# Chunked RWKV-7 recurrence: the 16x16 diagonal blocks of the triangular inverse move from matrix products to a block-per-partition substitution on VectorE, with two more pipeline stages

## The reference

```python
def step(state, inp):
    r_t, w_t, k_t, v_t, kk_t, a_t = inp
    sk = jnp.einsum('bhij,bhj->bhi', state, kk_t)
    state = (state * w_t[:, :, None, :]
             - sk[..., None] * (kk_t * a_t)[:, :, None, :]
             + v_t[..., None] * k_t[:, :, None, :])
    y = jnp.einsum('bhij,bhj->bhi', state, r_t)
    return state, y
```

## Time and profile before

| | |
|---|---|
| median of 3 runs | 3121.45 us (3116.18 to 3122.15) |
| profiled execution, its own time | 3126.26 us |
| span of the profiled execution | 3124.5 us |
| busy in the span: PE, DVE, ACT, POOL | 2800.0, 1582.2, 977.5, 1399.3 us |
| recurrence, from its first to its last work | about 1624 to 2261 us of the span |

### The profile page before, as it was taken

How to read it: one execution, slowest core, us unless ns; L and a number is a source line. 1 busy time by engine, 2 the same in 40 slices (tenths; PEclk the granted TensorE clock), 3 DMA queues, 4 the chain that set the end, 5 groups by cost and what they waited for, 6 DMA issues and landing times. The chain is left out here.

```text
span 3124.5 us, 58516 instructions
## 1 busy us (share of the span) xinstructions
PE 2800.0 (90%) x25184; PEld 2314.8 (74%) x25184; DVE 1582.2 (51%) x1939; ACT 977.5 (31%) x1703; POOL 1399.3 (45%) x742
## 2 busy tenths in 40 slices
PE   1787898999999999898978988888659999999999
PEld 1565676888877887677767887888647888878887
DVE  6744545656536343679635555555313543333344
ACT  2434433222232222445433333333224222222221
POOL 2532244444445444434435555656236444444443
PEclk9889999999999999999989999999879999999999
DMA  6421233544423232465651111111042222222223
GB/s 232 162 74 34 89 128 114 175 162 173 163 82 104 85 101 95 112 166 137 168 142 57 50 54 53 50 50 50 24 120 95 81 101 98 97 95 94 97 99 122
DMA packets 208642, 327.19 MB, mean 105 GB/s; under 512 B 126209, under 2 KB 126337, under 8 KB 208385
## 3 DMA queue, kind: packets, MB, share of 16 engines
q1 hardware_dynamic: 208384, 323.44, 32.5%
HBM read 288.86 MB, written 33.55 MB: 103 GB/s over the span
## 5 line engine op out<-in xcount | busy, mean ns | idle before, releaser
L687 POOL TENSOR_TENSOR wl<-w,wh 128x1024 fp32r<-128x1024 f32 x368 | 905.9, 2468 | 1305.0 <-ACT wh L728 1304.8
L180 PE MATMUL ps<-hi,wh 128*128 128x512 f32 x2208 | 883.8, 400 | 57.4 <-POOL wl L687 42.6
L181 PE MATMUL ps<-lo,wh 128*128 128x512 f32 x2208 | 870.0, 394 | 0.0
L182 PE MATMUL ps<-hi,wl 128*128 128x512 f32 x2208 | 869.5, 394 | 0.0
L728 ACT ACTIVATE wh<-w 128x1024 fp32r<-128x1024 f32 x368 | 388.1, 1056 | 708.3 <-DMA w<-in_ffn_w_in 527.7
L180 PEld LDWEIGHTS ps<-hi,wh 128*128 128x128 f32 x2208 | 420.4, 190 | 159.8 <-POOL wl L687 42.8
L994 DVE SCALAR_TENSOR_TENSOR xt<-ps,mod,xt 128x512 f32<-128x512 f32 x384 | 286.4, 750 | 437.7 <-PE ps L182 437.4
L181 PEld LDWEIGHTS ps<-lo,wh 128*128 128x128 f32 x2208 | 420.7, 191 | 89.5 <-issue 3.7
L182 PEld LDWEIGHTS ps<-hi,wl 128*128 128x128 f32 x2208 | 420.1, 190 | 90.0
L180 PE MATMUL ps<-act_hi,wh 128*128 128x512 f32 x704 | 282.2, 401 | 18.2 <-DVE act_lo L1003 9.7
L999 DVE TENSOR_TENSOR act<-ps,silu 128x512 f32<-128x512 f32 x88 | 60.8, 691 | 467.2 <-PE ps L182 467.2
(11 more groups left out here) (209 smaller groups left out, 3805.4 us busy)
## 6 DMA issues: line engine op xcount, KB each, us to landing
w<-in_ffn_w_in SPq DMA_DIRECT2D x176, 512.0 KB, 3.4
piece<-in_ada_w SPq DMA_DIRECT2D x96, 512.0 KB, 4.8
w<-in_ffn_w_out SPq DMA_DIRECT2D x88, 512.0 KB, 3.3
w<-in_w_rkv SPq DMA_DIRECT2D x48, 512.0 KB, 3.8
scratch<-silu SPq DMA_DIRECT2D x48, 256.0 KB, 2.9
scratch<-act SPq DMA_DIRECT2D x48, 256.0 KB, 2.9
w<-in_wqk SPq DMA_DIRECT2D x20, 512.0 KB, 5.0
xt<-in_xT SPq DMA_DIRECT2D x4, 2048.0 KB, 10.8
```

Of the source, the lines that this page charges most:

```text
L180: pe.matmul(out, w_hi(k), x_hi(k), start=first and k == 0, stop=False)
L181: pe.matmul(out, w_hi(k), x_lo(k), start=False, stop=False)
L182: ins = pe.matmul(out, w_lo(k), x_hi(k), start=False, stop=last and k == kc - 1)
L687: pool.tensor_tensor(wl[n % NW][:, :, :], wr[n % NW][:, :, :], wh[n % NW][:, :, :].bitcast(F32), ALU.subtract).then_inc(*wlo.up)
```

## The change

The inverse of the 16x16 diagonal blocks is no longer found by the levels 1, 2, 4 and 8 on PE. Instead, for chunk d:

- SP stores `n_t` to a DRAM image (`n_blocks`, 2 transfers), and reads the 64 diagonal blocks (16 heads x 4) back so that each lies in one partition of a 64-partition tile (`n_diag`, 8 transfers). One transfer takes 8 partitions, with 16 rows of 16 values each: 128 separate pieces of 64 bytes.
- DVE inverts all 64 blocks at once (`substitute`): doubling inside the partition, by broadcast products into `tmp` and sums over the last axis. These are 22 instructions, and each result is waited for by a semaphore.
- SP writes the inverses and their transposes into two further DRAM images (`t_blocks`, 16 transfers of 128 pieces of 64 bytes) whose other places were zeroed at the start, and loads the images as full tiles (`diag`, `diag_t`, 4 transfers).
- The levels 16 and 32 stay as they were, on PE, DVE and ACT, and start from these tiles. POOL masks only two levels, and the first inverse (L1378) is gone.

`period` now names five chunks: w = c+3 (loads, first key steps), x = c+2 (preparation), d = c+1 (diagonal blocks), y = c (two levels), zz = c-1 (solve and outputs). There are 20 periods, c from -3 to 16, in place of 16 with a `first` and a `last`. Tiles that live longer have three buffers (`RING`) in place of two. The core of the diff:

```diff
+                def periods(period):
+                    for c in range(-RING, NC + 1):
+                        period(at(c + 3), at(c + 2), at(c + 1), at(c), at(c - 1))
...
+                        def blocks_out(ch):
+                            b = ch % 2
+                            sp.wait_ge(*g["nt_done"].at(ch + 1))
+                            settle(sp)
+                            for h in range(2):
+                                sp.dma_start(image(n_img[b, h]), nt[b][h * HEAD:(h + 1) * HEAD, :, :]).then_inc(*n_out.up)
+                            sp.wait_ge(*n_out.at(2 * ch + 2))
+                            sp.wait_ge(*g["sub_done"].at(ch))
+                            for n in range(NX):
+                                h, n_h = divmod(n, NX // 2)
+                                sp.dma_start(nd[n * PAIRS:(n + 1) * PAIRS, 0:BLK * BLK].rearrange("p (r n) -> p r n", n=BLK),
+                                             diagonal(n_img[b, h], n_h)).then_inc(*nd_in.up)
+                        def blocks_back(ch):
+                            sp.wait_ge(*g["sub_done"].at(ch + 1))
...
+                            for n in range(NX):
+                                for w, x in enumerate((td, td_t)):
+                                    sp.dma_start(diagonal(t_img[b, w, h], n_h),
+                                                 x[rows, 0:BLK * BLK].rearrange("p (r n) -> p r n", n=BLK)).then_inc(*t_out.up)
+                            sp.wait_ge(*t_out.at(2 * NX * (ch + 1)))
+                            sp.wait_ge(*g["tr_done"].at(max(4 * ch - 6, 0)))
+                            for w, x in enumerate((tdiag, tdiag_t)):
+                                for h in range(2):
+                                    sp.dma_start(x[b][h * HEAD:(h + 1) * HEAD, :, :], image(t_img[b, w, h])).then_inc(*t_in[b].up)
...
+                        def small_product(out, left, right, size, count):
+                            shape = [DP, count, size, size, size]
+                            y = tmp[:, 0:count * size ** 3].rearrange("p (g i n k) -> p g i n k", i=size, n=size, k=size)
+                            for n in range(count):
+                                ins = dve.tensor_tensor(y[:, n], left[:, n].unsqueeze(2).to_broadcast([DP, size, size, size]),
+                                                        right[:, n].unsqueeze(1).to_broadcast([DP, size, size, size]), ALU.mult)
+                            step(ins)
+                            step(dve.tensor_reduce(out, y, AX.X, ALU.add))
...
+                        def period(w, x, d, y, zz):
+                            if zz is not None:
+                                solve_x(zz)
+                            if y is not None:
+                                level_x(y, 0), level_t(y, 0)
+                            if zz is not None:
+                                solve_u(zz)
+                            if y is not None:
+                                level_x(y, 1)
+                            if zz is not None:
+                                outputs(zz), state_products(zz)
+                            if y is not None:
+                                level_t(y, 1)
+                            if x is not None:
+                                by_token(x, 0), gram(x, 0), bonus_sums(x), by_token(x, 1)
+                            if zz is not None:
+                                by_feature(zz)
+                            if x is not None:
+                                gram(x, 1), by_token(x, 2)
+                            if w is not None:
+                                norms(w)
```

More of the change, by code:

```diff
@@ new lines, in _ @@
+                        for b in range(2):
+                            for w in range(2):
+                                for h in range(2):
+                                    sp.dma_start(image(t_img[b, w, h]), state[h * HEAD:(h + 1) * HEAD, :, :]).then_inc(*img_zero.up)
+                        def period(w, x, d, y, zz):
+                            if d is not None:
+                                blocks_out(d)
+                            if y is not None:
+                                load_gate(y)
+                            if w is not None:
+                                load_tiles(w)
+                            if d is not None:
+                                blocks_back(d)
@@ L1420, in _ @@
+                        periods(period)
                     @block.scalar
@@ new lines, in period @@
+                        def period(w, x, d, y, zz):
+                            if x is not None:
+                                norm_root(x)
+                            if y is not None:
+                                level(y, 0, 0), level(y, 0, 1)
+                            if x is not None:
+                                decays(x), end_decay(x)
+                            if y is not None:
+                                level(y, 1, 0), level(y, 1, 1)
+                            if x is not None:
+                                values_out(x)
+                            if zz is not None:
+                                square(zz)
+                            if x is not None:
+                                token_out(x, 0)
+                            if zz is not None:
+                                root(zz)
+                            if x is not None:
+                                token_out(x, 1)
+                            if w is not None:
+                                squares(w)
@@ L1498, in _ @@
                         act.wait_ge(*g["zeros"].at(1))
                         act.preload_act_table_set(LN_EXP)
-                        periods(act, first, period, lambda x: (square(x[0]), root(x[0])))
+                        periods(period)
                     @block.tensor
@@ L1651, in _ @@
                         pe.wait_ge(*g["zeros"].at(1))
-                        periods(pe, first, period, lambda y: (solve_x(*y), solve_u(*y), outputs(*y), state_products(*y), by_feature(y[0])))
+                        periods(period)
                     @block.vector
```

439 lines of the change are left out of this document (208 added, 231 removed).

## The result

Four runs of the changed kernel have a median of 3150.01 us (3146.25 to 3151.28), four of the kernel before 3121.8 us. The ratio is 1.009, with a 95% interval of 1.0077 to 1.0103: slower by 28 us. The prediction was 3138 with a range of 3095 to 3200, and slower as the likeliest sign. The measured time lies in the range, 12 us above the forecast.

The account below looks back on a forecast made before the run. PE's list set the old period; the new one, with pauses and slow clock, stays 37.5 us. 12 x 0 + 26.8 - 10 = +17 us on 3126.26 gives 3143, less 4.8 for the median: 3138, range 3095 to 3200.

Parts of the forecast that it names:

- it is there at 23.4: DVE's `y_centred`, behind the substitution, comes 23.4 us into the period; PE pauses 6.0 us before the bonus sums.
- the substitution: DVE's 22 new instructions: 3.05 us of columns, 2.65 of waiting ones, 0.55 of overlapping ones, 6.2 us in sum.
- the column price: On DVE, time from 512 to 1024 columns rises by 1.03 ns a column.
- the prediction's ladder: Stage time by length of DVE's substitution: 5.6 us gives 636, 6.2 gives 650, 7.0 gives 667, 8.0 gives 679.
- The clock: PE's groups behind the 6.0 us pause run slow: 3.8 us per period, at least nothing, at most 6.6.
- Filling and emptying: At the stage's start the first solve's copy comes 26.8 us later; at its end the last three intervals save 10.
- Busy times: Over the kernel, PE's busy time falls by some 120 us, POOL's by 105, DVE's rises by 45.
- The clock holds: Rival: PE's clock stays up despite the pause; period 33.7, stage 595, time 3083 us; chance 0.18, including nearly so.
- The way through DRAM is late: Rival: scatters and loads of d land after PE wants them, from 4.1 us over the layout; slower, 3173 or 3228; chance 0.20.
- The edges cancel: Rival: a 5.6 us substitution gives period 36.3 and stage 636, no change, 3124 us; chance 0.12.

Follow-up runs that it names:

- the two parts: Changed kernel with substitution sizes 1 to 4 before the new state, the 512-column products behind the decayed keys, and ACT's root before its `b_dec` copy: 3091.2 us.
- the products left out: Changed kernel without the substitution's 20 products and sums; the two copies and all DMAs stay, blocks are not inverted: 3025.42 us.
- The filled pause: Changed kernel with ten unused PE products added between the first Gram products and the bonus sums: 3120.58 us.
- 16 transfers more: Changed kernel with each of the 16 scatters repeated into a spare DRAM image that nothing reads, waited for like the others: 3182.54 us.
- the root first: Changed kernel with ACT taking the root for `y_norm` before it copies `b_dec` by token out: 3104.05 us.
- the substitution earlier: Changed kernel with DVE's whole substitution moved from behind the decayed keys of x to before the new state of zz: 3104.52 us.

## Why the prediction was right, and where its sizes were off

*The sign and the cause.* The step that decided was "it is there at 23.4. The pause is 6.0 us, so the clock falls". All of it is in the trace: 6.54 us, ended by `y_centred`, and a granted clock of 0.50 behind. Shortening the pause (the two parts, the products left out) or filling it moves the time each time in the direction that this gives. Counted from the start of `solve_x` (1941.92), in us:

| step ends | predicted | measured |
|---|---|---|
| decayed keys of x | 15.6 | 15.9 |
| first Gram products | 17.5 | 18.0 |
| substitution | 21.8 | 22.8 |
| `y_centred` | 23.4 | 24.4 |
| `b_dec` by token | 27.5 | 28.2 |
| `y_norm` | 29.5 | 30.0 |
| `k_dec` by token | 35.1 | 35.6 |
| norm sums, period | 37.5 | 37.8 |

(The parts that the prediction lists for its 37.5, from PE's list to the slow clock, add up to 37.3.)

*The term that was too small: the substitution.* 6.2 us were put down, 6.88 came. The two products of 512 columns last 1.01 and 1.06 us; the column price gave them 0.68, 0.53 for the columns and 0.15 fixed. That is 0.7 us, the whole difference. Their operands are read as 4-dimensional patterns, repeated and with rows and columns exchanged, and the sums over the same 512 columns keep to 0.68; that the patterns are the reason is likely but was not tested. For 7.0 us the prediction's ladder asked 34 us more of stage (667 against its 633 for the lists before). The trace has 23 more (660.4 against 637.0), since the intervals grew by only 0.6 us (7.0 us in 12).

*The clock.* 3.8 us per period were put down, on a period of 33.7 at full clock. The filled pause gives back 2.8 on average, but in five of its 12 intervals the clock still falls; against the other seven (34.7) the slow clock costs 3.5. So the period at full clock was laid out 1.0 us too short, 0.7 of it the substitution, and the clock 0.3 too dear. Together they make the 0.7 between 37.5 and 38.2.

*Filling and emptying.* +26.8 was predicted for the first solve, and it came 30.1 us later (1714.93 against 1684.78), but from there to the state update the changed kernel is 5.0 us quicker, so the update is 25.1 late. That the 26.8, taken for the solve and used for the update, came so near is in part luck. Of the 25.1, 1.2 us lie before any work of the stage: POOL's first memset is at 1626.0, where before it was at 1624.8. PE pauses 2.1 us before the first level 16, and not some 6. Emptying gave 6.8 back and not 10. In all: predicted +26.8 - 10 + 0 = +17, measured +25.1 - 6.8 + 7.0 = +25; the 3.2 us of emptying and the 7.0 of the intervals are the error, less 1.7 of filling. The other 3.5 of the 12 us are runs against medians: the profiled run before lay 4.8 above its median, which the prediction took off, and that of the changed kernel 1.3.

*Busy times.* PE fell by 101.5 us (predicted 120), POOL by 96.7 (105). DVE rose by 73.8 (45), of which 56 in the stage; the other 18 lie in phases that the change does not touch and were not looked into.

*The rivals.* "The clock holds": no, and the filled pause shows what it would have been worth, 3.5 us per period. "The way through DRAM is late": no; the scatters are issued every 0.37 us and not 0.47, and all have landed 1.2 us after the last. At 4.1 us (predicted) or 5 (measured) of margin it was near: 16 transfers more and PE waits, and without the products, at 29 us per period, PE waits too. "The edges cancel": they don't; the first solve alone comes 30 us later, and the substitution was longer than the 6.2 of the forecast and not shorter.

## What to carry to other kernels

When work leaves the engine that is the bound, ask what else stood behind its cover: here the levels on PE hid DVE's and ACT's chain, and what was taken from PE came back as pauses, then as slow clock. Lay the new lists out step by step before building, and look for the longest stretch in which one engine works alone; cutting that step in two and moving its first part to where its engine waited gave, with the root first, the fastest kernel of this study. Look at the chain behind a long pause as well: closing a pause of 1.85 us there, by exchanging two lines on ACT, gave twice its length per period and 46 us in all, and the same exchange gave nothing in the kernel before. And look at which wait ends last before adding two gains: with the substitution earlier, DVE's own list held `y_norm`, and the exchange gave nothing either.

## What the runs showed that was not expected

- 16 scatters of 128 pieces of 64 bytes cost SP 0.37 us each and had landed 1.2 us after the last issue; a store or load of 64 partitions x 512 columns cost 0.57 us to issue, more than the 0.42 to 0.44 of a full tile.
- The DVE products of 64x512 on rearranged and repeated operands took 1.01 and 1.06 us, sums over them 0.68.
- Four DVE products of 8 columns took 0.39 us with POOL idle and 2.27 beside its work.
- Exchanging root and copy brought the second Gram products from 2.4 to 3.6 us down to 1.92 although the long pause before them stayed the same.
- In the kernel with the filled pause the clock was at 1.00 into the pause of 1.85 us, and still fell in it or behind it in five periods of 12 (3.58 us for the Gram products at 1929.99) and stayed up in seven.
